# Differential attention: the second inverse as a step of its own, its product with lambda and part of the sum of 36 rows on GpSimd

## The reference, cut to what matters

```python
lam = (jnp.exp(jnp.sum(lq1 * lk1)) - jnp.exp(jnp.sum(lq2 * lk2)) + lambda_init)
def blk(qp, q1b, q2b):
    mask = _chunk_mask(qp, kpos)                       # causal by chunks of 64
    bias = jnp.where(mask[None], -slopes[:, None, None] * dist[None], NEG)
    s1 = jnp.einsum('bhqd,bhkd->bhqk', q1b, k1) * scale + bias
    s2 = jnp.einsum('bhqd,bhkd->bhqk', q2b, k2) * scale + bias
    a = jax.nn.softmax(s1, axis=-1) - lam * jax.nn.softmax(s2, axis=-1)
    return jnp.einsum('bhqk,bhkv->bhqv', a, v)
```

## Time and profile before

| | |
|---|---|
| median of 3 runs | 2601.74 us (2601.15 to 2602.24) |
| span of the profiled execution | 2600.7 us |
| the same execution against the median | 1.0 us less (the runs' times hold what lies around the span) |
| TensorE busy in the span | 2540.5 us (98%) |
| VectorE busy | 1614.7 us (62%) |
| ScalarE busy | 1212.5 us (47%) |
| GpSimd busy | 332.0 us (13%) |
| differential attention | from about 432 to 800 us |

### The profile page before, as it was taken

The page is one execution under the profiler, slowest core; times in us unless marked ns, Lnnn a source line. Parts: engine busy times, 40 slices in busy tenths (PEclk is TensorE's granted clock), DMA queues, the critical chain, the costliest instruction groups (busy, mean ns, idle before and its releaser), DMA issues.

```text
span 2600.7 us, 35372 instructions
## 1 busy us (share of the span) xinstructions
PE 2540.5 (98%) x12220; PEld 2114.9 (81%) x12220; DVE 1614.7 (62%) x3499; ACT 1212.5 (47%) x2183; POOL 332.0 (13%) x368
## 2 busy tenths in 40 slices
PE   8999999999999999999999999999999999999997
PEld 7998888777667999977877888888888888888886
DVE  6123306998995776654458677876757465564765
ACT  6112314777764555554544333533335353443554
POOL 1110002222221222210000000000000001111143
PEclk9999999999999999999999999999999999999999
DMA  7334458553332111135677767657655365776787
GB/s 232 122 106 125 126 163 253 143 135 87 93 131 90 36 31 45 41 110 158 194 247 220 221 200 237 218 182 216 190 161 179 110 221 108 171 167 162 203 162 137
DMA packets 329436, 398.59 MB, mean 153 GB/s; under 512 B 21408, under 2 KB 235664, under 8 KB 320944
## 3 DMA queue, kind: packets, MB, share of 16 engines
q1 hardware_dynamic: 311696, 364.41, 44.7%
q0 software_dynamic: 17568, 31.99, 8.4%
HBM read 239.86 MB, written 156.48 MB: 152 GB/s over the span
## 4 chain that ended last, share of the span: by engine, by line
PE 62%; DVE 3%; DMA 1%; ACT 1%; issue 1%; SPq 0%; POOL 0%; DVEq 0%; ACTq 0%; POOLq 0%
PE ff_ps_x L3262 26%; PE ff_ps_m L3262 13%; PE ff_ps_z L3262 6%; PE ml_ps_s L2139 6%; PE ff_ps_m L1695 4%; PE ml_ps_o L2168 4%; PE ml_ps_t L2152 2%; DMA ml_v_raw<-scr_yT 1%; DMA ff_pieces<-scr_acc 0%; PE ff_ps_r L2699 0%; PE mo_ps_t L2716 0%; SPq L2326 0%; DVE ff_pieces L2429 0%; DVE ff_pieces L2620 0%; DVE ff_pieces L2616 0%
## 5 line engine op out<-in xcount | busy, mean ns | idle before, releaser
L3262 PE MATMUL ff_ps_x<-ff_mv_hi_p,ff_st_hi_p 128*128 128x512 f32 x764 | 297.8, 390 | 0.5 <-ACT ff_u L3002 0.5
L3262 PE MATMUL ff_ps_x<-ff_mv_hi_p,ff_st_lo_p 128*128 128x512 f32 x764 | 297.3, 389 | 0.0
L3262 PE MATMUL ff_ps_x<-ff_mv_lo_p,ff_st_hi_p 128*128 128x512 f32 x764 | 297.2, 389 | 0.0
L2139 PE MATMUL ml_ps_s<-wide,ml_qs 128*128 128x416 f32 (+14 forms) x880 | 195.6, 356 | 3.7 <-PEq L137 2.7
L3108 DVE TENSOR_TENSOR ff_st_lo_p<-ff_ps_m,ff_st_hi_p 128x512 fp32r<-128x512 f32 x190 | 130.8, 689 | 103.4 <-ACT ff_st_hi_p L2985 103.4
L2952 POOL DMA_DIRECT2D scr_acc<-ff_pieces x64 | 55.5, 872 | 1015.3 <-DVE ff_pieces L3132 946.9
L3002 ACT ACTIVATE ff_u<-ff_ps_x 128x512 f32<-128x512 f32 x128 | 76.6, 598 | 215.0 <-PE ff_ps_x L3262 215.0
L3262 PEld LDWEIGHTS ff_ps_x<-ff_mv_hi_p,ff_st_hi_p 128*128 128x128 f32 x764 | 143.4, 188 | 32.4 <-issue 2.0
L3262 PEld LDWEIGHTS ff_ps_x<-ff_mv_hi_p,ff_st_lo_p 128*128 128x128 f32 x764 | 143.4, 188 | 29.9
L3262 PEld LDWEIGHTS ff_ps_x<-ff_mv_lo_p,ff_st_hi_p 128*128 128x128 f32 x764 | 143.4, 188 | 29.6
L2139 PEld LDWEIGHTS ml_ps_s<-wide,ml_qs 128*128 128x128 f32 x880 | 152.0, 191 | 16.3 <-issue 2.9
(11 more groups left out here) (318 smaller groups left out, 6349.7 us busy)
## 6 DMA issues: line engine op xcount, KB each, us to landing
st_raw<-in_w_ff SPq DMA_DIRECT2D x64, 512.0 KB, 6.2
scr_hid<-ff_pieces SPq DMA_DIRECT2D x128, 256.0 KB, 2.7
st_raw<-scr_hid SPq DMA_DIRECT2D x64, 512.0 KB, 5.4
ring<-in_w_ff SPq DMA_DIRECT2D x28, 1024.0 KB, 7.7
scr_t<-ring SPq DMA_DIRECT2D x24, 1024.0 KB, 5.8
ring<-scr_t SPq DMA_DIRECT2D x21, 1024.0 KB, 8.1
scr_acc<-ff_pieces POOLq DMA_DIRECT2D x64, 256.0 KB, 4.1
ring<-scr_u SPq DMA_DIRECT2D x13, 1024.0 KB, 8.4
```

The source lines that it names most:

```text
L2139: m = pe.matmul(ps_s[n % NSB][:, 0:w], q, k, start=j == 0, stop=j == len(pairs) - 1)
L3262: m = pe.matmul(bank[:, :], w[kind][:, k], a[kind][:, k], start=start and k == 0 and i == 0, stop=stop and k == KH - 1 and i == 2, skip_gr ...
```

## The change

The step "end" is split in three. The reciprocal of the second total becomes the step "second", two chunks behind the row's last chunk of component 1. Its product with minus lambda goes to GpSimd. For the 36 rows with i > 3 and i % 4 != 3 (nine in each of four heads), GpSimd also takes the first 40 per cent of the columns (rounded down to a multiple of 32) of the sum, as a product in place and an addition; VectorE's SCALAR_TENSOR_TENSOR covers the rest. VectorE waits for GpSimd's share before the buffer of the second map is written again, TensorE before a group's first transpose. The cost of "end" in the planner falls by the share.

```diff
+        SHARE = 40
+        def share(i):
+            return 0 if i % 4 == 3 or i < 4 else SHARE * (META + P * (i + 1)) // 100 // 32 * 32
+        SHARED = [i for i in range(NT) if share(i)]
+        def shares_until(h, i):
+            return len(SHARED) * h + sum(1 for a in SHARED if a <= i)
...
                         if c == COMPS - 1:
+                            later.append((SCALE_AFTER, ("second", 0, i)))
                             later.append((END_AFTER, ("end", 0, i)))
...
-            return META + P * (step[2] + 1) + 250 if step[0] == "end" else 0
+            return META + P * (step[2] + 1) - share(step[2]) + 250 if step[0] == "end" else 0
...
+            def second_inverse(h, i, u, **at):
+                if isinstance(h, int) and (h, i) == (0, 0):
+                    pool.wait_ge(lam_made, 2)
+                hold(pool, second_inv_ready, NT * h + i + 1)
+                pool.tensor_scalar(inv2[:, i % 2:i % 2 + 1], inv[:, i % 2, 1:2], lam[:, 3:4], 1.0, ALU.mult, ALU.mult).then_inc(inv2_ready, 1)
+                if share(i):
+                    part, other = row(i, u)[:, 0:share(i)], comp_row(i, 1, u)[:, 0:share(i)]
+                    pool.wait_ge(inv2_ready, NT * h + i + 1)
+                    pool.tensor_scalar(other, other, inv2[:, i % 2:i % 2 + 1], 1.0, ALU.mult, ALU.mult).then_inc(share_scaled, 1)
+                    pool.wait_ge(first_scaled, NT * h + i + 1)
+                    pool.wait_ge(share_scaled, shares_until(h, i))
+                    pool.tensor_tensor(part, part, other, ALU.add).then_inc(share_done, 1)
...
             def chunk(h, n, pair, u):
+                if c == 1 and k0 == 0 and not (first_head and not shares_until(0, i - 2)):
+                    dve.wait_ge(share_done, shares_until(h, i - 2))
...
-            def end(h, i, u, **at):
+            def invert_second(h, i, u, **at):
                 if isinstance(h, int) and (h, i) == (0, 0):
                     minus_lambda()
-                n = 2 * (NT * h + i)
                 dve.wait_ge(exp_ready, NT * COMPS * h + COMPS * (i + 1))
-                dve.reciprocal(inv[:, i % 2, 1:2], total[:, i % 2, 1:2]).then_inc(inv2_step, 1)
-                dve.wait_ge(inv2_step, n + 1)
-                dve.tensor_scalar(inv2[:, i % 2:i % 2 + 1], inv[:, i % 2, 1:2], lam[:, 3:4], None, ALU.mult).then_inc(inv2_step, 1)
-                dve.wait_ge(inv2_step, n + 2)
+                dve.reciprocal(inv[:, i % 2, 1:2], total[:, i % 2, 1:2]).then_inc(second_inv_ready, 1)
+            def end(h, i, u, **at):
+                rest = slice(share(i), META + P * (i + 1))
+                dve.wait_ge(inv2_ready, NT * h + i + 1)
                 dve.wait_ge(first_scaled, NT * h + i + 1)
-                dve.scalar_tensor_tensor(out=row(i, u), in0=comp_row(i, 1, u), scalar=inv2[:, i % 2:i % 2 + 1], in1=row(i, u),
-                                         op0=ALU.mult, op1=ALU.add).then_inc(probs_ready, 1)
+                dve.scalar_tensor_tensor(out=row(i, u)[:, rest], in0=comp_row(i, 1, u)[:, rest], scalar=inv2[:, i % 2:i % 2 + 1],
+                                         in1=row(i, u)[:, rest], op0=ALU.mult, op1=ALU.add).then_inc(probs_ready, 1)
...
             def turn(h, g, t, u, **at):
                 if t == 0:
                     pe.wait_ge(probs_ready, NT * h + 4 * g + 4)
+                    if g:
+                        pe.wait_ge(share_done, shares_until(h, 4 * g + 3))
```

More of the change, by code:

```diff
@@ L1201, in attention @@
         scores_ready, scores_read = mem.sem("da_scores_ready"), mem.sem("da_scores_read")
+        second_inv_ready, share_scaled = mem.sem("da_second_inv_ready"), mem.sem("da_share_scaled")
+        inv2_ready, share_done, lam_made = mem.sem("da_inv2_ready"), mem.sem("da_share_done"), mem.sem("da_lam_made")
         max_ready, exp_ready = mem.sem("da_max_ready"), mem.sem("da_exp_ready")
         inv_ready, first_scaled, probs_ready = (mem.sem(f"da_{s}") for s in ("inv_ready", "first_scaled", "probs_ready"))
-        inv2_step = mem.sem("da_inv2_step")
         pT_ready, pv_done = mem.sem(f"da_pT_ready"), mem.sem("da_pv_done")
@@ L1469, in scaled @@
                 pool.tensor_scalar(row(i, u), row(i, u), inv[:, i % 2, 0:1], 1.0, ALU.mult, ALU.mult).then_inc(first_scaled, 1)
-            heads(pool, {"scale": scaled})
+            def second_inverse(h, i, u, **at):
[10 more added lines that the diff above has]
+                    pool.tensor_tensor(part, part, other, ALU.add).then_inc(share_done, 1)
+            heads(pool, {"scale": scaled, "second": second_inverse})
         @stage.scalar
@@ L1551, in minus_lambda @@
                 dve.wait_ge(lam_exp, 2)
[L1552 to L1555, removed]
+                dve.tensor_tensor(lam[:, 2:3], lam[:, 1:2], lam[:, 0:1], ALU.subtract).then_inc(lam_made, 1)
+                dve.wait_ge(lam_made, 1)
+                dve.tensor_scalar(lam[:, 3:4], lam[:, 2:3], -LAMBDA_INIT, None, ALU.add).then_inc(lam_made, 1)
             def invert(h, i, u, **at):
@@ L1563, in invert @@
                 dve.reciprocal(inv[:, i % 2, 0:1], total[:, i % 2, 0:1]).then_inc(inv_ready, 1)
-            def end(h, i, u, **at):
+            def invert_second(h, i, u, **at):
                 if isinstance(h, int) and (h, i) == (0, 0):
                     minus_lambda()
-                n = 2 * (NT * h + i)
                 dve.wait_ge(exp_ready, NT * COMPS * h + COMPS * (i + 1))
-                dve.reciprocal(inv[:, i % 2, 1:2], total[:, i % 2, 1:2]).then_inc(inv2_step, 1)
-                dve.wait_ge(inv2_step, n + 1)
-                dve.tensor_scalar(inv2[:, i % 2:i % 2 + 1], inv[:, i % 2, 1:2], lam[:, 3:4], None, ALU.mult).then_inc(inv2_step, 1)
-                dve.wait_ge(inv2_step, n + 2)
+                dve.reciprocal(inv[:, i % 2, 1:2], total[:, i % 2, 1:2]).then_inc(second_inv_ready, 1)
+            def end(h, i, u, **at):
+                rest = slice(share(i), META + P * (i + 1))
+                dve.wait_ge(inv2_ready, NT * h + i + 1)
                 dve.wait_ge(first_scaled, NT * h + i + 1)
-                dve.scalar_tensor_tensor(out=row(i, u), in0=comp_row(i, 1, u), scalar=inv2[:, i % 2:i % 2 + 1], in1=row(i, u),
-                                         op0=ALU.mult, op1=ALU.add).then_inc(probs_ready, 1)
-            heads(dve, {"chunk": chunk, "scale": invert, "end": end})
+                dve.scalar_tensor_tensor(out=row(i, u)[:, rest], in0=comp_row(i, 1, u)[:, rest], scalar=inv2[:, i % 2:i % 2 + 1],
+                                         in1=row(i, u)[:, rest], op0=ALU.mult, op1=ALU.add).then_inc(probs_ready, 1)
+            heads(dve, {"chunk": chunk, "scale": invert, "second": invert_second, "end": end})
             dve.wait_ge(probs_ready, NT * H)
```

## The result

The changed kernel takes 2607.96 us (median of 7 runs, 2605.71 to 2611.03) against 2601.15 us of the kernel before in the same job; ratio 1.0028, 95% interval 1.0017 to 1.0039. That is 6.8 us slower. The forecast was 2603.3 us with a range of 2591 to 2612. A second job gave 2606.85 against 2600.01, ratio 1.0031 (1.0021 to 1.0041).

A forecast was written before the change was run, and what follows sets the result against it. TensorE and VectorE, both nearly full, were taken to bound the stage. Per head +0.5 us from row 10 on, less 0.1 from rows 8 and 9, gave +0.4, four heads +1.6: 2603.3 us, range 2591 to 2612.

The forecast's parts named there:

- the likeliest case: Whole kernel: row 14's sum meets GpSimd's addition, other rows gain a little; 2603.3 us, alone 2600 to 2607; chance 0.38.
- the rival in which row 13 is caught: GpSimd's addition holds up row 13's sum as well: 1.6 us a head, 6.4 in all, 2609.7 us; chance 0.20.
- What bounds the stage, and the ceiling: Differential attention stage: TensorE and VectorE nearly full; only TensorE's waits for VectorE, 12.7 us, can be given back.
- The early reciprocal: Second reciprocal waits for ScalarE's exponential in rows 8 to 14: 1.0 us in row 14, about 5 us a head.
- The meeting at the port: Row 14: VectorE's sum, reading SBUF twice, waits for GpSimd's addition and ends 1.3 us later than before.
- The first rival, no meeting: Sums and GpSimd's additions never meet: -1.5 us a head, four times -6, 2595.7 us; chance 0.20.
- The others: Ends of sums against before: row 12 -0.2, 11 -0.2, 10 -0.3, 9 0, 8 -0.1, 15 +0.17 us.
- costed the planner at 0: Planner's lower cost of a sum shifts transposes or products: under 0.3 us in either direction, taken as 0.
- Rows 0 to 7 cost nothing: Rows 0 to 7: TensorE is the later engine and four score banks cover some 1.5 us of delay, so nothing.
- The sum: All row terms together: +0.4 us a head, +1.6 us over four heads, 2603.3 us.

The follow-up runs named there:

- the late kernel: Changed kernel with the step "second" one chunk ahead of the end of the sum's row instead of two chunks behind: 2598.87 us, ratio 0.9998.

## Why the prediction was right, and where it was not

The time of 2607.96 us lies in the range of 2591 to 2612, but outside the 2600 to 2607 of the likeliest case, and near the 2609.7 of the rival in which row 13 is caught. That rival did not come true: row 13 was caught in one head of four, and other terms made up the difference. The mechanism was right; that the time fell within the range is in part luck, for the sum behind it was short by a factor of three to four.

*What bounds the stage, and the ceiling.* Not contradicted: no version got under the kernel before by more than 5.4 us, with TensorE's waits for score banks all but gone (0.8 us) and those for the row sums left.

*The early reciprocal.* Right: it waits 1.01 us in row 14 (1.0 forecast) and 0.70 in row 13 (0.7); over the stage the wait grew by 24.2 - 6.7 = 17.5 us, 4.4 a head (about 5). The run without shares prices it at 15 us, with the way over GpSimd in it.

*The meeting at the port.* Right in mechanism and place: row 14 in every head, its sum 2.97 us long, shown by the run that leaves the addition out. Mis-sized by 0.2 us (row end +1.52, forecast +1.3). Two terms were short: the one-column product takes 0.27 us on GpSimd, not 0.19, with 0.36 to the next start instead of 0.29; and the addition of 768 columns takes 1.82 us, not 1.69. I had drawn a line through additions of different operands; the two new forms above give (1823 - 733) / 512 = 2.13 ns a column. (The Trainium skill, page "GPSIMD Engine Reference", section "Performance versus the Vector engine", has about 2.6 cycles an element for an addition with two inputs. With the 1.2 GHz of the same section that makes an estimate of 2.17 ns: these rows agree.)

*Row 13.* Named as a rival decided at 0.1 us; it went my way in three heads (row end -0.27 us) and the other way in the first (+1.51), where a chunk started 0.33 us late behind the reciprocal and the sum came 0.10 us too late. That is 1.8 us in all: 1.4 by the port and 0.4 by the late chunk, which is there without the addition too (row end +0.10). What the chunk waited for stays open.

*The first rival, no meeting.* Its price of -6 us was too good: with the addition left out the time was 2598.28 against 2600.01 us, less than 2 us under the kernel before. In that run sums still met GpSimd's product (rows 8 and 9, 1.27 and 1.32 us for 720 and 784 columns, 0.97 and 1.03 in the late kernel).

*The others.* Row 12 -0.28 (-0.2 forecast), row 11 -0.15 (-0.2), row 10 -0.18 (-0.3), row 8 -0.11 (-0.1), row 15 +0.18 (+0.17). Row 9 was wrong in three heads: +0.42 instead of 0, because its exponential starts 0.45 us later behind a copy of transposed tiles, whose place in time the planner's new cost had moved; I had costed the planner at 0. In the total that 0 is not refuted, since the old cost won nothing.

*"Rows 0 to 7 cost nothing".* Right in the net, wrong in the rows. In the second to fourth head rows 0 to 3 each take 0.17 to 0.36 us longer, by the way over GpSimd; rows 4 to 7 give it back, row 6 alone 0.75 us. From the end of row 15's sum to that of row 7 it is -0.1 to +0.1 us a head. That four score banks cover 1.5 us, as the forecast has it, no run tested.

*The sum.* +0.4 a head and 1.6 in all were forecast. The profiles show +1.3 to +1.5 in the second to fourth head. Counted from the end of one row's sum to the next, what the forecast lacked is 0.4 to 0.5 us in rows 8 and 9, 0.2 in row 14 and 0.1 each in rows 10 and 12. The first head has +2.8 from the stage's start (row 13 adds 1.8, and row 9 costs 0.6 less), so that the last row 15 is 6.9 us late; 2.2 of these the start of the latent stage gives back, which the forecast did not have. The stage so costs 4.7 us in the profiles against the 1.6 forecast, and 6.8 us in the medians. The sign was right, the size forecast a third to a quarter of the measured one. With runs of one kernel 7 us apart, one execution can't settle the difference between 4.7 and 6.8.

## What to carry to other kernels

Work that is handed from VectorE to GpSimd must be read with its operands: if both engines then read SBUF (VectorE with two operands), the one that comes second waited here for nearly the whole instruction of the first (all but 0.15 to 0.2 us of the overlap), and the order should be arranged so that the instruction off the critical path is the one that comes second. A step that is moved earlier to give another engine a start must not come before what it waits for is done: here two chunks were too early by 1 us in row 14, four were right, and the move alone, without a column less work on VectorE, made the kernel 15 us slower with the early step (its product on GpSimd) and 3.5 us slower with the late one (its product then on VectorE). Fewer busy microseconds on a full engine are no gain until the waits that come with them are priced in the same rows.

## What the runs showed of the hardware that I had not expected

- The port goes by hundredths of a microsecond, and the same way each time: VectorE's sum issued 0.09 to 0.11 us behind GpSimd's addition of 1.7 to 1.8 us waited for it to the end in both profiles of the changed kernel, while one that waited already during GpSimd's product got in between product and addition, a gap of 0.15 us (591.84 + 0.91 to 592.90 in the kernel with the late step).
- A TENSOR_SCALAR of one column takes 0.27 us on GpSimd in this stage (mean of 64) and took 0.19 us in a later one (1127.80). The operands differ; why the times do was not followed.
- GpSimd's reported time of an addition includes its wait for the port: 704 columns read 1.70 us free and 2.67 us behind a sum.
